# A new order for the opening of a four-layer stack: first norm, first modulation and bias load rearranged

## What is computed

```python
silu_c, silu_cc = silu(c), silu(c_ctx)
mod_lat = silu_c @ ada_w[0] + ada_b[0]          # 1024 x 6144
mod_ctx = silu_cc @ ada_w[0] + ada_b[0]
sh1, sc1, g1, sh2, sc2, g2 = split(mod_lat, 6)
h_lat = rmsnorm(x, norm_g[0, 0]) * (1 + sc1) + sh1      # and h_ctx from ctx
q, k, v, u, g = split(h_lat @ w_in, ...)
bias = rpb[:, dr, dc]      # (8, 15, 31), gathered by row and column distance
s_nb = where(in_window, q k^T * scale + bias, -1e30)    # neighbourhood attention
```

## Time and profile before

| | |
|---|---|
| median of 3 runs | 2147.91 us (2146.45 to 2150.86) |
| profiled execution, its own time | 2149.46 us |
| its span, first to last instruction | 2147.7 us |
| mean granted TensorE clock | 0.974 |
| busy share of the span: PE, DVE, ACT, POOL | 92%, 57%, 43%, 22% |
| bytes moved, mean rate | 296.89 MB, 138 GB/s |

### The profile page before, as it was taken

The page is one execution under the profiler, slowest core; times in us unless marked ns, Lnnn a source line. Parts: engine busy times, 40 slices in busy tenths (PEclk is TensorE's granted clock), DMA queues, the critical chain, the costliest instruction groups (busy, mean ns, idle before and its releaser), DMA issues.

```text
span 2147.7 us, 34211 instructions
## 1 busy us (share of the span) xinstructions
PE 1985.9 (92%) x13391; PEld 1747.7 (81%) x13391; DVE 1233.6 (57%) x1698; ACT 921.1 (43%) x1433; POOL 483.2 (22%) x452
## 2 busy tenths in 40 slices
PE   3999969999999889999979997999889999989998
PEld 1677647777777669989969996998889999879997
DVE  0545455542455554657567675756675566787464
ACT  2634425322332342148456454336643334564333
POOL 3200013430343100012014141000027360006281
PEclk9999989999999999999989998999999999999999
DMA  9531323446442213222324544542244454324553
GB/s 306 184 118 60 118 98 137 159 164 213 163 155 81 86 61 136 79 79 98 125 94 166 177 163 137 183 158 99 85 149 168 168 176 157 109 74 172 177 183 112
DMA packets 44721, 296.89 MB, mean 138 GB/s; under 512 B 5232, under 2 KB 6512, under 8 KB 12592
## 3 DMA queue, kind: packets, MB, share of 16 engines
q1 hardware_dynamic: 36432, 245.38, 33.5%
q10 hardware_dynamic: 6336, 44.65, 6.1%
q0 software_dynamic: 1824, 5.02, 0.8%
HBM read 293.99 MB, written 1.05 MB: 137 GB/s over the span
## 4 chain that ended last, share of the span: by engine, by line
PE 73%; DVE 8%; POOL 7%; issue 5%; ACT 4%; DMA 2%; SPq 0%; POOLq 0%; DVEq 0%; ACTq 0%
PE acc L453 19%; PE acc L455 19%; PE acc L454 19%; POOL hid L1698 2%; POOL Fhi L1699 2%; DMA w_raw<-in_w_hyb_g 2%; PE acc L448 2%; PE wk L564 2%; PE acc L449 2%; PE acc L450 2%; DVE w_lo L390 2%; PE wk L1498 1%; POOL Flo L1702 1%; PE wk L585 1%; ACT w_hi L380 1%
## 5 line engine op out<-in xcount | busy, mean ns | idle before, releaser
L453 PE MATMUL acc<-Hhi,w_hi 128*128 128x272 f32 (+2 forms) x2304 | 744.6, 323 | 43.8 <-DVE Hlo L746 24.1
L390 DVE TENSOR_TENSOR w_lo<-w_raw,w_hi 128x1024 fp32r<-128x1024 f32 (+2 forms) x472 | 606.9, 1324 | 232.1 <-ACT w_hi L380 231.1
L455 PE MATMUL acc<-Hhi,w_lo 128*128 128x272 f32 (+2 forms) x2304 | 720.2, 313 | 0.0
L454 PE MATMUL acc<-Hlo,w_hi 128*128 128x272 f32 (+2 forms) x2304 | 719.7, 312 | 0.0
L380 ACT ACTIVATE w_hi<-w_raw 128x1024 fp32r<-128x1024 f32 (+2 forms) x472 | 452.6, 1006 | 439.4 <-PE acc L455 354.7
L453 PEld LDWEIGHTS acc<-Hhi,w_hi 128*128 128x128 f32 x2304 | 440.4, 191 | 91.1 <-issue 46.4
L455 PEld LDWEIGHTS acc<-Hhi,w_lo 128*128 128x128 f32 x2304 | 439.9, 191 | 22.4
L454 PEld LDWEIGHTS acc<-Hlo,w_hi 128*128 128x128 f32 x2304 | 440.6, 191 | 21.5 <-issue 0.2
L453 PE MATMUL acc<-Fhi,w_hi 128*128 128x256 f32 (+2 forms) x864 | 268.2, 310 | 10.5 <-POOL Flo L1702 5.6
L455 PE MATMUL acc<-Fhi,w_lo 128*128 128x256 f32 (+2 forms) x864 | 266.6, 309 | 0.0
L454 PE MATMUL acc<-Flo,w_hi 128*128 128x256 f32 (+2 forms) x864 | 266.3, 308 | 0.0
(11 more groups left out here) (360 smaller groups left out, 2546.5 us busy)
## 6 DMA issues: line engine op xcount, KB each, us to landing
w_raw<-in_w_ffn_in SPq DMA_DIRECT2D x44, 1024.0 KB, 4.8
ada_ring<-in_w_ada ACTq DMA_DIRECT2D x40, 1024.0 KB, 4.8
w_raw<-in_w_mlp_in SPq DMA_DIRECT2D x32, 1024.0 KB, 4.8
w_raw<-in_w_mlp_out SPq DMA_DIRECT2D x32, 1024.0 KB, 4.8
w_raw<-in_w_ffn_out SPq DMA_DIRECT2D x32, 704.0 KB, 4.1
ada_first<-in_w_ada SPq DMA_DIRECT2D x8, 1024.0 KB, 30.9
w_raw<-in_w_ret_v SPq DMA_DIRECT2D x8, 1024.0 KB, 4.8
w_raw<-in_w_ret_g SPq DMA_DIRECT2D x8, 1024.0 KB, 4.8
```

The lines of the kernel that those rows point to most:

```text
L390: dve.tensor_tensor(w_lo[:, r, a:b], w_raw[:, r, a:b], w_hi[:, r, a:b].bitcast(F32), ALU.subtract).then_inc(lo_done, 1)
L453: pe.matmul(o, w_hi[:, r, w], x_hi(k), start=k == 0, stop=False)
L454: pe.matmul(o, w_hi[:, r, w], x_lo(k), start=False, stop=False)
L455: mm = pe.matmul(o, w_lo[:, r, w], x_hi(k), start=False, stop=k == last)
```

## The change

- SP issues X first, then the eight ada slots in the order 0, 4, 1, 5, 2, 6, 3, 7, so that each pair holds the shift and the scale of the same two chunks, with weight slot 0 ahead of the last pair. Each ada slot has a place of its own that leaves H_hi free.
- The squares are summed over chunks on DVE (sq_acc), and PE makes one sum over the partitions.
- Modulation is made in four pairs: PE two products and two columns, DVE shifts and gains of two chunks. Behind each pair ACT and DVE make two chunks of H: ACT the context half and the rounding, DVE the scaling, the x half and H_lo. The split of weight slot 0 follows the second pair on ACT and the third on DVE.
- The flip matrix, the 16 loads, the flip matmuls and copies go. The host lays the bias out as the tile wants it, and POOL loads it straight into rpb in one piece, once PE has used all eight ada slots; the late constants are issued behind it, and the ada ring's first loads move on ACT behind the first norm, under the same wait.
- Numbers of the semaphores for gains and shifts are shifted to fit four first groups instead of one.

```diff
-        ada_first = [at("ada_first0", [P, 4, SLOT], A), at("ada_first1", [P, 4, SLOT], h0)]
+        ada_first = [at(f"ada_first{i}", [P, SLOT], o) for i, o in enumerate(
+            (nt0 + 18 * KB, A + 50 * KB, A, A + 8 * KB, A + 16 * KB, A + 24 * KB, A + 34 * KB, A + 42 * KB))]
...
+                    if g == 0:
+                        continue
...
-        CONSTS = [("ones", ones), ("flip", flip)]
+        CONSTS = [("ones", ones)]
...
-            act.dma_start(X[:, :, :], t["x"]).then_inc(s_x, 16)
...
         def load_biases(pool):
 
-
-            rows = t["na_rpb"].tensor
-            for s in range(2):
-                for h in range(8):
-                    src = bass.AP(rows, h * 465 + (5 - s) * 31 + 15 - 63, [[1, GRID_W], [31, 6], [1, GRID_W]])
-                    pool.dma_start(rpb_up[64 * s:64 * s + 64, h, :, :], src).then_inc(s_bias, 16)
+            pool.wait_ge(ada_used, ADA_FIRST)
+            pool.dma_start(rpb[:, :, :, :], t["rpb"]).then_inc(s_bias, 16)
...
-        def load_ada_first(sp):
+        def ada_slot(s):
+
+            return s // 2 + 4 * (s % 2) if s < ADA_FIRST else s
+
+        def load_opening(sp):
+
+            sp.dma_start(X[:, :, :], t["x"]).then_inc(s_x, 16)
             for s in range(ADA_FIRST):
-                sp.dma_start(ada_first[s // 4][:, s % 4, :], t["w_ada"][s]).then_inc(ada_loaded[s // 2], 16)
+                if s == ADA_FIRST - 2:
+                    sp.dma_start(w_raw[:, 0, 0:layers[0].width], t["w_" + layers[0].name][0]).then_inc(w_loaded[0], 16)
+                sp.dma_start(ada_first[s][:, :], t["w_ada"][ada_slot(s)]).then_inc(ada_loaded[s // 2], 16)
 
         def load_ada_ring(act):
-            act.wait_ge(s_flip, 6)
+            act.wait_ge(ada_used, ADA_FIRST)
             for r in range(2):
...
-                if g == 0:
-                    pe.wait_ge(s_flipped, 6)
...
+            if s < ADA_FIRST and s % 2 == 0 and s > 0:
+                pe.wait_ge(s_mod, s // 2)
             for c in range(2):
-                m = 2 * s + c
+                m = 2 * ada_slot(s) + c
                 mm = pe.matmul(wk[:, 3, 2 * m:2 * m + 2], ada_rows_of(s)[:, c * P:(c + 1) * P], V("pad", 0, 2),
                                start=True, stop=True)
             mm.then_inc(ada_done, 1)
 
         def pe_ada_first(pe):
-            for s in range(ADA_FIRST + 1):
-                if s < ADA_FIRST:
+            for i in range(ADA_FIRST // 2):
+                for s in (2 * i, 2 * i + 1):
                     pe_ada_products(pe, s)
-                if s >= 1:
-                    pe_ada_columns(pe, s - 1)
+                for s in (2 * i, 2 * i + 1):
+                    pe_ada_columns(pe, s)
...
-        def dve_mod_first(dve, link):
-            dve.wait_ge(ada_done, ADA_FIRST)
-            dve_mod(dve, link, 0, 0, 16, [0])
+        def dve_mod_first(dve, i):
+
+            def pair(x):
+                return x.rearrange("p (a m) s -> p a m s", a=2)[:, :, 2 * i:2 * i + 2, :]
+            bias = V("ada_b", 0, 16).rearrange("p (m s) -> p m s", s=1).to_broadcast([P, 16, 2])
+            dve.wait_ge(ada_done, 2 * i + 2)
+            dve.tensor_tensor(pair(mod[:, 0, 0:16, :]), pair(wk[:, 3, 0:32].rearrange("p (m s) -> p m s", s=2)), pair(bias),
+                              ALU.add).then_inc(s_mod, 1)
+            dve.wait_ge(s_mod, i + 1)
+            for s in range(2):
+                ins = dve.scalar_tensor_tensor(gains[:, 0, 0, s, 2 * i:2 * i + 2], mod[:, 0, 8 + 2 * i:10 + 2 * i, s], 1.0,
+                                               V("norm_g", 2 * i, 2), ALU.add, ALU.mult)
+            ins.then_inc(s_gain, 1)
...
+        def pe_first_norm(pe):
+            pe.wait_ge(s_const, N_CONST)
+            pe.wait_ge(nsq_used, DC)
+            pe.matmul(wk[:, 0, :], ones[:, :], sq_acc[:, :], start=True, stop=True).then_inc(s_sum, 1)
+
+        def act_first_norm(act):
+
+            def hi(i):
+                act.wait_ge(s_gain, i + 1)
+                for c in (2 * i, 2 * i + 1):
+                    act.wait_ge(nt_ready, c + 1)
+                    if c >= 2:
+                        act.wait_ge(h_ready, c - 1)
+                    s, a, b = BOTH[0]
+                    act.activation(n32[:, c % 2, a:b], nt[:, c % 2, a:b], ACT.Identity, scale=ada_gain(0, 0)(s, c),
+                                   bias=ada_shift(0, 0)(s, c)).then_inc(n32_ctx, 1)
+                for c in (2 * i, 2 * i + 1):
+                    act.wait_ge(n32_ctx, c + 1)
+                    act.wait_ge(n32_ready, c + 1)
+                    act.activation(H_hi[T1][:, c, :], n32[:, c % 2, :], ACT.Copy).then_inc(hhi_ready, 1)
+            act.wait_ge(s_vec, 16)
+            act.wait_ge(s_x, 16)
+            for c in range(DC):
+                if c >= 2:
+                    act.wait_ge(nsq_used, max(c - 1, 2))
+                act.activation(sq[:, c % 2, :], X[:, c, :], ACT.Square).then_inc(nsq_ready, 1)
+            act.wait_ge(s_sum, 1)
+            act.activation(root[:, :], wk[:, 0, :], ACT.Sqrt, bias=V("eps"), scale=1.0 / D).then_inc(root_ready, 1)
+            act_ada(act, 0, 4)
+            hi(0)
+            act_ada(act, 4, 6)
+            hi(1)
+            split_first(act)
+            act_ada(act, 6, 8)
+            hi(2)
+            hi(3)
+
+        def dve_first_norm(dve):
+            for c in range(1, DC):
+                dve.wait_ge(nsq_ready, c + 1)
+                if c > 1:
+                    dve.wait_ge(nsq_used, c)
+                dve.tensor_tensor(sq_acc[:, :], sq[:, 0, :] if c == 1 else sq_acc[:, :], sq[:, c % 2, :], ALU.add)\
+                    .then_inc(nsq_used, 2 if c == 1 else 1)
+            dve.wait_ge(root_ready, 1)
+            dve.reciprocal(rstd[:, :], root[:, :]).then_inc(rstd_ready, 1)
+            dve.wait_ge(rstd_ready, 1)
+
+            def scaled(c):
+                if c >= 2:
+                    dve.wait_ge(n32_ctx, c - 1)
+                dve.tensor_tensor(nt[:, c % 2, :], X[:, c, :], rstd[:, :], ALU.mult).then_inc(nt_ready, 1)
+            scaled(0)
+            scaled(1)
+            for i in range(4):
+                dve_mod_first(dve, i)
+                dve.wait_ge(s_gain, i + 1)
+                for c in (2 * i, 2 * i + 1):
+                    dve.wait_ge(nt_ready, c + 1)
+                    if c >= 2:
+                        dve.wait_ge(hhi_ready, c - 1)
+                    s, a, b = BOTH[1]
+                    dve.tensor_scalar(n32[:, c % 2, a:b], nt[:, c % 2, a:b], ada_gain(0, 0)(s, c), ada_shift(0, 0)(s, c),
+                                      ALU.mult, ALU.add).then_inc(n32_ready, 1)
+                if i < 3:
+                    for c in (2 * i + 2, 2 * i + 3):
+                        dve.wait_ge(n32_ready, c - 1)
+                        scaled(c)
+                for c in (2 * i, 2 * i + 1):
+                    dve.wait_ge(hhi_ready, c + 1)
+                    dve.tensor_tensor(H_lo[T1][:, c, :], n32[:, c % 2, :], H_hi[T1][:, c, :].bitcast(F32),
+                                      ALU.subtract).then_inc(h_ready, 1)
+                if i == 2:
+                    split_first(dve)
...
-        def pe_rpb(pe, first, last):
-
-            flat = rpb_up[:, :, :, :].rearrange("p h j k -> p (h j k)")
-            pe.wait_ge(s_bias, N_BIAS)
-            pe.wait_ge(root_ready, 1)
-            for b in range(first, last):
-                if b >= 3:
-                    pe.wait_ge(s_flipped, b - 2)
-                pe.matmul(wk[:, b % 3, :], flip[:, :], flat[:, b * 512:(b + 1) * 512], start=True, stop=True)\
-                    .then_inc(s_flip, 1)
-
-        def act_rpb(act, first, last):
-            flat = rpb[:, :, :, :].rearrange("p h j k -> p (h j k)")
-            for b in range(first, last):
-                act.wait_ge(s_flip, b + 1)
-                act.activation(flat[:, b * 512:(b + 1) * 512], wk[:, b % 3, :], ACT.Copy).then_inc(s_flipped, 1)
-
         def pool_rpb(pool, link):
 
-            pool.wait_ge(s_flipped, 6)
+            pool.wait_ge(s_bias, N_BIAS)
...
-            load_ada_first(sp)
+            load_opening(sp)
...
-            act_norm(act, 0, meanwhile=lambda: (act_ada(act, 0, 6), split_first(act), act_ada(act, 6, ADA_FIRST)))
-            act_rpb(act, 0, 3)
-            act_gelu(act, "hyb_g", g_sb, after=lambda s: (act_rpb(act, 3, 6), load_ada_ring(act)) if s == 0 else None)
+            act_first_norm(act)
+            load_ada_ring(act)
+            act_gelu(act, "hyb_g", g_sb)
             act_hyb_first(act)
...
-            dve_norm(dve, 0, meanwhile=lambda: (split_first(dve), dve_mod_first(dve, link)))
+            dve_first_norm(dve)
...
-            pe_norm(pe, 0)
+            pe_first_norm(pe)
             pe_ada_first(pe)
-            pe_rpb(pe, 0, 3)
             hyb = (lambda k: H_hi[T1][:, k, :], lambda k: H_lo[T1][:, k, :])
-            project(pe, "hyb_g", *hyb, need=h_need(pe, 0), after=lambda s: pe_rpb(pe, 3, 6) if s == 0 else None)
```

(46 more changed lines are left out.)

## The result

The changed kernel took 2132.82 us in the median (2128.08 to 2134.02) against 2148.22, a ratio of 0.9924 (95% interval 0.9909 to 0.9939): 15.4 us faster, 0.7%. The forecast was 2128.1, with a range of 2120 to 2139. The profiled execution took 2134.02, its span was 2132.0.

What follows compares the result with a forecast made beforehand. PE bounds most of the span, but the load stream sets the opening; the second slot of hyb_g starting at 56 instead of 75.8 us saves 19.8, from the median 2147.91 to 2128.1 us, range 2120 to 2139.

Steps and rivals of the forecast that it cites:

- The bound: Whole kernel: PE carries 73% of the span, but the opening waits 47.84 us on the first weight slot's load.
- Loads: Opening: 12.1 MB without small pieces stream at 412 GB/s instead of 275; X lands at 10 us, last pair at 33.
- T: Time at which the last ada pair lands in the opening: 33 us, or 48 at 275 GB/s.
- The norm's chain: Norm beside the loads: reciprocal done at 23.3 us, then 3.7 per pair of chunks, second pair at 32.0.
- From T to the projection: Last pair's landing to hyb_g's first matmul: 7 us of work plus 2 of clock, so start at 42.
- the half clock: PE at half speed after idling: products charged 2 us more, the projection's start 1.8 us more.
- Second slot: Start of hyb_g's second weight slot: 55 us, or 56 with 1 us for the selects, against 75.8 before.
- the selects: POOL's four bias-masking selects beside DVE's passes during hyb_g: charged 1 us, bounds 0 and 3.
- Moved loads: Bias and late constants, issued from 37 us, land between 58 and 68; transposes want them at 67: hidden, narrowly.
- Rivals B and C: Late constants hold PE at the transposes: B partly, 2138 us, chance 0.10; C in full, slower, 2153 us, chance 0.03.
- Sum: Opening up to hyb_g's second slot: 75.8 - 56 = 19.8 us saved, giving 2128.1 against the median.
- one of my signs of being wrong: Stages behind the attention differing by more than a microsecond from before would count against the forecast.

Runs made afterwards that it cites:

- e_small: Changed kernel with the 16 old bias loads (256-byte pieces, never read) and eight late constants issued at the start again; 2147.76 us, ratio 0.9992.
- e_consts: Changed kernel with eight of the ten late constants issued at the very start, without the 16 bias loads; 2133.71 us, ratio 0.9927.
- e_bias: Kernel before with only the bias part: host layout, one late load, constants behind it, no flip work; old norm and modulation; 2137.82 us, ratio 0.9952.
- e_best: Changed kernel with DVE's split of weight slot 0 earlier, twelve idle-time PE matmuls and POOL's selects held back; 2122.03 us, ratio 0.9884.
- e_warm2: Changed kernel with DVE's split of weight slot 0 earlier and twelve idle-time PE matmuls, second measurement; 2119.98 us, ratio 0.9872.

## Why the prediction was right

**The bound.** Right. The load's end set the opening before and after, at 47.84 + 5.07 and at 33.68.
**Loads.** 412 GB/s taken, 421 measured; T at 33 forecast, 33.7 measured; X at 10, forecast and measured. e_small shows that the term depends on what rides under the large loads; e_consts shows that I lumped too much together as small pieces: the late constants didn't lower the rate, the 16 bias loads did.
**The norm's chain.** Reciprocal done at 23.3 forecast, 24.0 measured; the second pair of chunks was done at 32.0 forecast, 33.6 measured, because the first pair took 4.7 us (25.3 to 30.0) instead of 3.7. I had the norm 1 us ahead of T; it was 0.1 us ahead. PE's idle 2.41 us before T are no measure of it, since PE had nothing left to do of the first three pairs. Loads that came much earlier would have gained little: ACT was done with w_hi at 34.4 and copied the last pair's first row at 35.3.
**From T to the projection.** 7 + 2 us of clock forecast (to 42), 8.0 measured (to 41.71): the products lost 1.4 us to the half clock instead of 2.
**Second slot.** Forecast 56. Its first matmul, the 49th behind 41.71, started at 55.5, so the first slot took 13.8 us: 10.9 for 48 matmuls at 0.23 and 2.9 for the clock (fourteen of them at 0.43). I had 11.3, read from a stretch that holds 52 matmuls, and 1.8. The mis-sized terms are these: the slot itself 0.4 too long, the half clock 2.9 in the slot instead of 1.8 and 1.4 in the products instead of 2, T 0.7 too early, and the selects 0 instead of 1. They nearly cancel, and that they do is luck; the mechanism is the one forecast. The trace agrees with the lock that the Trainium skill states (SBUF — State Buffer, section Who interferes with whom): in e_bias each two-input pass of DVE ended behind a select, and it cost 8.8 us at the transposes (78.78 against 69.98). In the changed kernel I had its size per pass; the slack of what it held back was larger than my sum made it.
**Moved loads.** The last constant landed at 42.80 + 14.0 = 56.8, wanted at 67.8; I had 58 to 68. Rivals B and C didn't occur; e_best and e_warm2 show B's point to be near 60 us. The rule of the Trainium skill on starved descriptors that the prediction cites (SBUF — State Buffer, section SBUF: two separate sides) speaks of DVE passes in a two-port mode. No view here shows which passes run in one, so no run tests it; POOL's queue moved 3.18 MB between 36 and 50 us while DVE worked.
**Sum.** 19.8 forecast; 20.2 at the transposes and, at the end, 15.4, 20.8 and 20.5 in the three comparisons. The first profile lost its 4.5 us in later stages, so one of my signs of being wrong (stages behind the attention that differ by more than a microsecond) was there; the repeats show it to be a difference between executions of one kernel and no term of the sum. Half-speed stretches go with it at the places looked at. Over all thirteen executions the median is 2128.1, equal to the forecast; the first four alone gave 2132.8.
**What I didn't separate.** My sum took the change as one. The runs show that the bias part (its loads, and the flip matmuls on PE) is worth 18.0 us if the selects are kept away from the norm, and 10.0 if not; the new order of norm and loads adds 2.2 us to the first (67.76 against 69.98) and 10.2 to the second, because it has all but two of the norm's eight chunks done before the selects start. On its own, with the bias loads still in the stream, it brings nothing (e_small).

## What to carry to other kernels

In an opening that only loads, count what small pieces ride under the large ones, and test them by size: 1.57 MB in pieces of 256 bytes took the stream from about 415 to 277 GB/s and cost 14.7 us, while 1.27 MB in pieces of 512 to 2176 bytes cost hardly more than their bytes. Laying that one table out on the host, and issuing it and the late constants later, was worth most of the gain. When such work moves, look at which other engine it then takes turns with, and at which loads a faster engine calls up early. When an engine's wait is unavoidable, a dozen idle matmuls on PE can be cheaper than the half-speed stretch behind it.

## What I had not expected of the hardware

POOL's selects and DVE's two-input passes don't merely slow one another, they take turns: over 11 us in e_bias each of four passes of 0.69 us took between 2.50 and 2.93. And two profiles of one kernel, which agreed to 0.05 us up to 940 us, differed by 4 at their ends; at a place where both had waited 2.3 us, one was granted 0.83 of the clock over the next stretch and the other 1.00.
